# Final RMS norm of a decoder block: root by ScalarE, reciprocal by VectorE, and three of eight tiles multiplied by the gain on GpSimd

## The reference, cut to what matters

```python
def rms_norm(x, g):
    x32 = x.astype(jnp.float32)
    y = x32 * lax.rsqrt(jnp.mean(x32 * x32, axis=-1, keepdims=True) + EPS)
    return (y * g.astype(jnp.float32)).astype(x.dtype)
...
        x = x + hierarchical_moe(v, ...)      # every token gets two weighted expert rows
    return rms_norm(x, g_final)
```

## Time and profile before

| | us |
|---|---|
| median of three runs | 1853.19 |
| lowest and highest run | 1851.72, 1853.20 |
| span of the profiled execution, first to last instruction | 1850.8 |
| PE busy in the span | 1715.4 |
| DVE busy in the span | 1038.1 |
| ACT busy in the span | 842.7 |
| POOL busy in the span | 140.3 |

### The profile page before, as it was taken

One profiled execution on the slowest core, in us unless ns is written; L12 is line 12 of the kernel. 1 busy time (PEld: TensorE's weight loads), 2 busy tenths in 40 slices (PEclk: granted clock), 3 DMA queues, 4 the chain that ended last, 5 costly groups with the idle time before them and its releaser, 6 DMA issues. The chain is left out here.

```text
span 1850.8 us, 22586 instructions
## 1 busy us (share of the span) xinstructions
PE 1715.4 (93%) x8515; PEld 1369.1 (74%) x8515; DVE 1038.1 (56%) x1125; ACT 842.7 (46%) x845; POOL 140.3 (8%) x187
## 2 busy tenths in 40 slices
PE   5999999999999998988888999959999999999991
PEld 4888888889987887867776889846667777777760
DVE  4353534442214113246665432769998888888886
ACT  5433434241221312135453111237778777777772
POOL 1000000000000000011110000010000000000005
PEclk9999999999999999999998999969999999999995
DMA  4242333223332323545644250179999999999977
GB/s 149 92 153 91 112 114 126 93 99 137 137 115 68 110 95 114 193 153 197 213 148 165 91 186 23 63 284 398 393 399 394 393 398 393 399 392 393 399 285 280
DMA packets 151685, 390.36 MB, mean 211 GB/s; under 512 B 14008, under 2 KB 73480, under 8 KB 147536
## 3 DMA queue, kind: packets, MB, share of 16 engines
q1 hardware_dynamic: 138368, 343.20, 50.3%
q0 software_dynamic: 8384, 29.63, 5.1%
q10 hardware_dynamic: 4880, 16.82, 2.3%
HBM read 322.15 MB, written 67.46 MB: 211 GB/s over the span
## 5 line engine op out<-in xcount | busy, mean ns | idle before, releaser
L1608 DVE TENSOR_TENSOR e_l<-e_raw,e_h 128x2048 fp32r<-128x2048 f32 x192 | 439.2, 2290 | 65.6 <-ACT e_h L1602 65.3
L1602 ACT ACTIVATE e_h<-e_raw 128x2048 fp32r<-128x2048 f32 x192 | 367.8, 1917 | 85.5 <-PE ps L1637 50.1
L199 PE MATMUL ps<-uh,w_h 128*128 128x512 f32 x1008 | 313.1, 392 | 11.9 <-DVE ul L908 9.7
L199 PE MATMUL ps<-ul,w_h 128*128 128x512 f32 x1008 | 312.0, 391 | 0.0
L199 PE MATMUL ps<-uh,w_l 128*128 128x512 f32 x1008 | 311.7, 390 | 0.0
L183 DVE TENSOR_TENSOR w_l<-w_raw,w_h 128x2048 fp32r<-128x2048 f32 x38 | 87.1, 2291 | 328.6 <-ACT w_h L179 328.6
L199 PEld LDWEIGHTS ps<-uh,w_h 128*128 128x128 f32 x1008 | 190.1, 189 | 52.8 <-issue 13.2
L199 PEld LDWEIGHTS ps<-ul,w_h 128*128 128x128 f32 x1008 | 190.5, 189 | 40.0
L199 PEld LDWEIGHTS ps<-uh,w_l 128*128 128x128 f32 x1008 | 190.1, 189 | 39.7
L1624 PE MATMUL ps<-e_h,e_xth 128*96 128x512 f32 x512 | 205.3, 401 | 6.3 <-DVE e_l L1608 3.0
L1624 PE MATMUL ps<-e_h,e_xtl 128*96 128x512 f32 x512 | 202.8, 396 | 0.0
(11 more groups left out here) (285 smaller groups left out, 2439.8 us busy)
## 6 DMA issues: line engine op xcount, KB each, us to landing
e_raw<-w_exp_gate SPq DMA_DIRECT2D x64, 1024.0 KB, 19.5
e_raw<-w_exp_up SPq DMA_DIRECT2D x64, 1024.0 KB, 19.2
e_raw<-w_exp_down SPq DMA_DIRECT2D x64, 1024.0 KB, 18.9
w_raw<-w_in SPq DMA_DIRECT2D x28, 1024.0 KB, 5.5
qk_d<-qk SPq DMA_DIRECT2D x16, 1024.0 KB, 4.2
at_qk<-qk_d SPq DMA_DIRECT2D x8, 2048.0 KB, 10.8
y_d<-e_y ACTq DMA_DIRECT2D x32, 384.0 KB, 6.4
y_d<-zeros POOLq DMA_DIRECT2D x22, 384.0 KB, 4.2
```

The costliest lines, as they stand in the source:

```text
L199: mm = pe.matmul(ps[:, h * HALF:(h + 1) * HALF], w[:, k, :], u[:, k, h * HALF:(h + 1) * HALF], start=first, stop=last)
L1602: act.activation(self.e_h[m % SPLIT][:, :, :], self.e_raw[slot][:, :, :], ACT.Copy).then_inc(self.e_hi[m % SPLIT], 1)
L1608: dve.tensor_tensor(self.e_l[slot][:, :, :], self.e_raw[slot][:, :, :], self.e_h[m % SPLIT][:, :, :].bitcast(F32), ALU.subtract).then_inc( ...
```

## The change

The norm's chain of small steps is divided anew. ScalarE's square is scaled by D ** -0.5, so its sum is already the mean; ScalarE then takes the root of mean plus EPS (the EPS comes from a new 128x1 tile `small`), and VectorE takes the reciprocal. GpSimd's power is gone. For tiles 1, 3 and 5 (`SHARED`) VectorE no longer computes the norm: ScalarE multiplies `x2` by rstd into `far`, and GpSimd multiplies that by g_final in place. SyncE waits for GpSimd's product at these tiles and stores in the same order as before.

```diff
+        small = final.put("cb_small", [P, 1])
...
+        small_set = sem("cb_small_set")
+        SHARED, ROOT = (1, 3, 5), D ** -0.5
...
                 for t in range(NT):
-                    sp.wait_ge(normed, t + 1)
+                    shared = sum(u <= t for u in SHARED)
+                    if t in SHARED:
+                        sp.wait_ge(gained, shared)
+                    else:
+                        sp.wait_ge(normed, t + 1 - shared)
                     sp.dma_start(k_.out[t * P:(t + 1) * P, :], far[t][:, :]).then_inc(out_stored, 16)
...
                 pool.memset(power[:, :], -0.5).then_inc(const, 1)
+                pool.memset(small[:, :], EPS).then_inc(small_set, 1)
...
-                    pool.tensor_tensor(mean[:, :], power[:, :], power[:, :], ALU.mult).then_inc(surplus_ready, 1)
+                    pool.tensor_tensor(total[:, :], power[:, :], power[:, :], ALU.mult).then_inc(surplus_ready, 1)
...
-                pool.tensor_tensor(rstd[:, :], power[:, :], power[:, :], ALU.mult).then_inc(const, 1)
+                pool.tensor_tensor(total[:, :], power[:, :], power[:, :], ALU.mult).then_inc(const, 1)
                 pool.wait_ge(const, 2)
                 for t in range(NT):
                     rows(LATER, t, far, far_in)
-                for t in range(NT):
-                    pool.wait_ge(averaged, t + 1)
-                    pool.tensor_tensor(rstd[:, t:t + 1], mean[:, t:t + 1], power[:, t:t + 1], ALU.pow).then_inc(powered, 1)
+                pool.wait_ge(g_in, 16)
+                for n, t in enumerate(SHARED):
+                    pool.wait_ge(scaled, n + 1)
+                    pool.tensor_tensor(far[t][:, :], far[t][:, :], g_b[:, :], ALU.mult).then_inc(gained, 1)
...
+                act.wait_ge(small_set, 1)
                 for t in range(NT):
                     act.wait_ge(added, t + 1)
-                    act.activation(near[t][:, :], k_.x2[:, t, :], ACT.Square, accum_out=total[:, t:t + 1]).then_inc(squared, 1)
+                    act.activation(near[t][:, :], k_.x2[:, t, :], ACT.Square, scale=ROOT, accum_out=mean[:, t:t + 1]).then_inc(squared, 1)
+                    act.wait_ge(squared, t + 1)
+                    act.activation(rstd[:, t:t + 1], mean[:, t:t + 1], ACT.Sqrt, bias=small[:, :]).then_inc(rooted, 1)
+                    if t - 2 in SHARED:
+                        act.wait_ge(powered, t - 1)
+                        act.activation(far[t - 2][:, :], k_.x2[:, t - 2, :], ACT.Copy,
+                                       scale=rstd[:, t - 2:t - 1]).then_inc(scaled, 1)
...
-                def average(t):
-                    dve.wait_ge(squared, t + 1)
-                    dve.tensor_scalar(mean[:, t:t + 1], total[:, t:t + 1], 1.0 / D, EPS, ALU.mult, ALU.add).then_inc(averaged, 1)
+                def root(t):
+                    dve.wait_ge(rooted, t + 1)
+                    dve.reciprocal(rstd[:, t:t + 1], rstd[:, t:t + 1]).then_inc(powered, 1)
 
                 def norm(t):
+                    if t in SHARED:
+                        return
                     dve.wait_ge(powered, t + 1)
...
```

More of the change, by code:

```diff
@@ L1669, in experts @@
         near_in, far_in = ([sem(f"cb_{n}_in{t}") for t in range(NT)] for n in ("near", "far"))
-        g_in, const, surplus_ready, near_added, surplus_added, added, squared, averaged, powered, normed, out_stored = (
-            sem("cb_" + n) for n in ("g", "const", "surplus_ready", "near_added", "surplus", "added", "squared", "averaged", "powered", "normed", "stored"))
+        g_in, const, surplus_ready, near_added, surplus_added, added, squared, rooted, powered, scaled, gained, normed, out_stored = (
+            sem("cb_" + n) for n in ("g", "const", "surplus_ready", "near_added", "surplus", "added", "squared", "rooted", "powered", "scaled", "gained", "normed", "stored"))
+        small_set = sem("cb_small_set")
+        SHARED, ROOT = (1, 3, 5), D ** -0.5
         by_chunk = lambda ps: ps.rearrange("p (k t) -> p k t", t=P)[:, :, 0:BLK]
@@ L2097, in _ @@
                     if t >= 1:
-                        average(t - 1)
+                        root(t - 1)
                     if t >= 2:
                         norm(t - 2)
-                average(NT - 1)
+                root(NT - 1)
                 for t in (NT - 2, NT - 1):
```

## The result

| | us |
|---|---|
| before, median of 14 runs | 1851.43 (1846.49 to 1854.15) |
| changed, median of 14 runs | 1857.18 (1852.49 to 1859.84) |
| ratio changed to before, 95% interval | 1.0031, 1.0021 to 1.0041 |
| span of the profiled execution, changed | 1855.2 (before: 1850.8) |

The change makes the kernel slower, by 0.31% or 5.7 us (interval 3.9 to 7.6). Between the two profiled executions it is 4.4 us. By that measure it is 1850.8 - 1822.66 = 28.1 before and 1855.2 - 1822.43 = 32.8 after: +4.6.

The account below looks back on a forecast made before the run. VectorE was taken to bound the closing part from the first norm on. Added waits and bunched stores, 0.7 + 2.2 + 1.3, gave +4.2 us: 1853.2 + 4.2 = 1857.4, range 1852.2 to 1859.5.

Parts of the forecast that it names:

- the sum: Closing part, change in us: 0.7 up to add 7, 2.2 from the third product, 1.3 from bunched stores; +4.2.
- The step on which the sign hangs: Closing part: GpSimd's product, reading SBUF, makes VectorE's next instruction with two tiles wait for the whole 2.3 us.
- The product: GpSimd's 128x1024 multiplication by g_final on a shared tile: 2.3 us, range 1.94 to 2.68.
- The end: Last stores: tiles 5, 6 and 7 follow back to back, 1.3 us each, span ends 1.6 later; bunching adds 1.3.
- The root's half: Root on ScalarE instead of GpSimd's power: 2.59 us of idle time before norm 0 goes; one table load, 1.30 us.
- Side by side: Rival, closing part: GpSimd's product does not hold VectorE; -0.8 us, not slower; chance 0.21.
- Starving: Rival: VectorE keeps its turn, GpSimd's products squeeze in where it waits for roots; +0.7 to +5.2 us; chance 0.07.
- Tables in turns: Rival: square and root lie in different ScalarE tables, every tile costs two loads; +16 us; chance 0.06.
- the order of the stores: SyncE stores in order, so tile 5's late product bunches three stores; most of VectorE's gain is lost in any case.

Follow-up runs that it names:

- writes only: Changed kernel with GpSimd's product on tiles 1, 3 and 5 replaced by two memsets, gain and scaled values left out; run once, 1854.24 us.
- gain in PSUM: Changed kernel with g_final copied once to PSUM by ScalarE and read there by VectorE's norms; ratio to the kernel before 1.0018.
- halves: Changed kernel with each GpSimd product written as two instructions of 512 columns; run once, 1857.15 us.
- share only: Kernel before with only the sharing of tiles 1, 3 and 5; the power stays on GpSimd, product t-2 behind power t; ratio 1.0035.
- root only: Changed kernel with no tile shared: root on ScalarE, reciprocal and all eight norms on VectorE; ratio to the kernel before 0.9988.
- root only with norm 6 first: The kernel with no tile shared, norm 6 moved ahead of root 7 in VectorE's program; ratio to the kernel before 0.9994, again 0.9989.

## Why the prediction was right, point by point

- **The time.** Forecast 1857.4, measured 1857.18; forecast end of the span 1855.0, found 1855.2. The kernel before measured 1.8 us lower over 14 runs than over the three on which the forecast stood, so the measured difference, 5.7, is larger than the forecast 4.2. The interval (3.9 to 7.6) includes both the forecast 4.2 and the 4.6 of the traces. That the two absolute times agree to 0.2 is luck: two differences of 1.5 and 1.8 cancel, and so do two errors of the sum, below.
- **The step on which the sign hangs** was right, and is now shown and not only argued. A GpSimd product holds VectorE's next instruction with two tiles from SBUF; memsets hold nothing, and a norm with one tile from PSUM isn't held. The rule of the Trainium skill, SBUF — State Buffer, section "Who interferes with whom", is borne out in the direction that the trace of before could not show: 3.37 us instead of 1.28. The page writes "fully blocks" of VectorE's two-port modes, and of two inputs in SBUF only that they contend with GpSimd's reads under an exclusive lock; here such an instruction was held until the product ended.
- **The product** was put at 2.3, bounds 1.94 and 2.68; it takes 2.34 to 2.47. But it holds VectorE only 2.09, since its first 0.2 us lie beside the end of the norm before. Three times 0.2 accounts for most of what the sum had too much: norm 7 ends 2.3 later after add 0 than before, not 3.0.
- **The end** was undersized. I gave 1.3 us to three bunched stores; the time from norm 7 to the end grew by 2.3 (3.8 to 6.2). The step that is too small is the 1.6 us from the end of the data to the end of the span: the data of the three stores ran at full rate from 1848.8 to 1852.7, the 3.9 of the sum, and the span ended 2.5 later. The two errors, -0.7 and +1.0, nearly cancel, so the total is better than its terms.
- **The root's half.** Norm 0 came 2.2 us earlier after add 0 (5.6 instead of 7.8); the root took 0.29 (0.26 assumed), the table load 1.28 and came once. The first accumulator read ends at 1824.97, the load starts at 1824.98 and the root at 1826.28: again no drain beside it, and the Trainium skill, ScalarE: Activation LUTs, section "What ACT_TABLE_LOAD costs", has 2.66 us for what took 1.30.
- **The rivals.** Side by side is out by 3.37 against 1.28. Starving is out: every product started within 0.2 us of ScalarE's copy and ran at once. Tables in turns is out: one load. That the order of the stores takes back VectorE's gain even without any hold was right; "writes only" shows it: norm 7 ends 3.6 us earlier after add 0, and the closing part is only 0.4 shorter.

## What to carry to other kernels

Don't give GpSimd an operation that reads SBUF tiles while VectorE, with two SBUF tiles per instruction, is the bound: each product held VectorE for 2.1 us to save it 1.2, and the third saved it nothing. What was seen to run undisturbed beside the other engine's reads was a VectorE instruction with one of its two tiles in PSUM, and what disturbed nobody was a GpSimd instruction that only writes. Neither made sharing pay here: gain in PSUM closed 3.9 us later than the kernel before, and writes only, which leaves the gain out, 0.4 earlier. And when a share of an ordered sequence goes to a slower engine, keep it away from the last tiles: the third product cost 4.4 us, the other two 2.4 together.

## What the runs showed of the hardware that was not expected

**Held time is booked as busy.** The 2.1 us appear in no wait of the profile; only the duration of a group's longest member, or busy time that rises though work was taken away, gives them away.

**Three stores, bunched.** When stores 5, 6 and 7 were issued together, the span ended 6.3 us after GpSimd's last product (gain in PSUM 1849.25 to 1855.6, halves 1849.22 to 1855.5). When store 7 came about 1.1 us after store 5, it ended 7.3 us after (changed kernel 1847.94 to 1855.2, share only 1850.92 to 1858.2), although data moved at about 400 GB/s until 1852.5 in the changed kernel (the last two columns are the DMA share and GB/s):

```profile
1852.00:1852.50 0.50, 0.00 (x0) 0.00 (x0) 0.00 (x0) 0.00 (x0) 0.00 (x0) 0.50 1.05 401
1852.50:1853.00 0.50, 0.00 (x0) 0.00 (x0) 0.00 (x0) 0.00 (x0) 0.00 (x0) 0.50 0.37 139
1853.00:1853.50 0.50, 0.00 (x0) 0.00 (x0) 0.00 (x0) 0.00 (x0) 0.00 (x0) 0.50 0.08 33
```

A small rest comes late. In windows of 0.1 us the full rate ends at 1852.7, and single packets trickle in until 1853.5; the span ends 1.7 later. In share only it is the same, 1855.7 and 1856.5. In gain in PSUM there is no such rest: full rate until 1854.0, and the end 1.6 later, as before the change (1849.2 to 1850.8). Writes only, whose three stores were issued together too, lies between: 6.7 us after the last memset, with a rest of 0.4 us. So the issue times alone do not explain it. Why it happens was not tried; it is what made the end longer than forecast.

**The wait for the last expert rows varies.** From the issue of the last `y_d` store to the order-point product behind it, GpSimd needed 5.6 us in the kernel before (1811.31 to 1816.92), 5.9 in the changed one, 6.0 in root only and 8.4 in root only with norm 6 first (1811.97 to 1820.35); that same kernel traced again needed 7.5, and the others lie between 6.5 and 7.8. The change does nothing there but let the order-point product write another tile. It is probably a part of the 8 us over which runs of one kernel spread, and the reason for reading these experiments from add 0 on; what sets it stays open. Of the kernel before there is only one trace, and its wait is the shortest of all, so a loss of a few tenths of a us ahead of add 0 (the 0.6 above) is not excluded.
